# Forget gate's product: from the three-pass scheme to fp32 on quarters of TensorE's columns, with VectorE's chain split behind two k tiles and a third PSUM slot for the turnings

## The reference, cut to what matters

```
def run_layer(x, pos, ...):
    h = rmsnorm(x, norm_mix_g)
    z = h @ w_in
    u_pool = z[..., COL_POOL:COL_SSM]
    u_ssm = z[..., COL_SSM:COL_Q]
    q = z[..., COL_Q:COL_K].reshape(bn, L, FOX_HEADS, FOX_HEAD_DIM)
    k = z[..., COL_K:COL_V].reshape(bn, L, FOX_HEADS, FOX_HEAD_DIM)
    v = z[..., COL_V:COL_F].reshape(bn, L, FOX_HEADS, FOX_HEAD_DIM)
    logf = jax.nn.log_sigmoid(z[..., COL_F:COL_GATE].astype(jnp.float32)
                              + b_f.astype(jnp.float32))
    ...
    c_all = jnp.cumsum(logf_all, axis=1)
```

## Time and profile before

| | us |
|---|---|
| three runs | 1794.1, 1788.59, 1792.3 |
| median | 1792.3 |
| the profiled execution, its own time | 1792.1 |
| its span (first to last instruction of the trace) | 1790.3 |
| mean granted TensorE clock | 0.991 of full speed |
| busy in the span | PE 97%, PEld 93%, DVE 70%, ACT 36%, POOL 37% |

### The profile page before, as it was taken

The page is one execution under the profiler, slowest core; times in us unless marked ns, Lnnn a source line. Parts: engine busy times, 40 slices in busy tenths (PEclk is TensorE's granted clock), DMA queues, the critical chain, the costliest instruction groups (busy, mean ns, idle before and its releaser), DMA issues.

```text
span 1790.3 us, 31528 instructions
## 1 busy us (share of the span) xinstructions
PE 1738.6 (97%) x12453; PEld 1673.7 (93%) x12453; DVE 1246.4 (70%) x1913; ACT 641.5 (36%) x1234; POOL 668.2 (37%) x471
## 2 busy tenths in 40 slices
PE   7999999999998999999999989999999999999997
PEld 7999999888878989989999979999999999999997
DVE  6788663676775577553574589777777777698685
ACT  4210013565652222251002344444444444534343
POOL 4554334333354667413223223555544454000000
PEclk9999999999999999999999999999999999999999
DMA  8634728665634554366546331322222221998252
GB/s 275 184 123 131 235 99 251 173 174 155 177 98 139 137 115 93 90 194 216 181 133 188 95 105 37 93 89 73 73 73 73 73 73 62 348 345 284 89 189 89
DMA packets 249316, 260.69 MB, mean 146 GB/s; under 512 B 50674, under 2 KB 202974, under 8 KB 248723
## 3 DMA queue, kind: packets, MB, share of 16 engines
q1 hardware_dynamic: 235042, 227.49, 42.8%
q10 hardware_dynamic: 14128, 31.21, 4.9%
HBM read 178.09 MB, written 76.09 MB: 142 GB/s over the span
## 4 chain that ended last, share of the span: by engine, by line
PE 53%; DVE 6%; DMA 4%; issue 3%; ACT 2%; POOL 1%; SPq 0%; POOLq 0%; ACTq 0%; DVEq 0%
PE bank L156 49%; DMA act_raw<-act_scratch 2%; DMA down_raw<-in_w_down 2%; PE bank L1951 1%; PE bank L2762 1%; PE bank L1966 0%; DVE x_forms L3039 0%; PE bank L1971 0%; DVE merged L2252 0%; DMA gate<-gate_scratch 0%; DVE conv L3119 0%; POOL up_forms L2603 0%; PE bank L1936 0%; DVE xt L3009 0%; DVE prod L2245 0%
## 5 line engine op out<-in xcount | busy, mean ns | idle before, releaser
L156 PE MATMUL bank<-act_hi,w_hi 128*128 128x364 f32 (+1 forms) x1296 | 438.0, 338 | 5.2 <-DVE act_lo L2130 2.2
L156 PE MATMUL bank<-act_lo,w_hi 128*128 128x364 f32 (+1 forms) x1296 | 427.3, 330 | 0.0
L156 PE MATMUL bank<-act_hi,w_lo 128*128 128x364 f32 (+1 forms) x1296 | 426.7, 329 | 0.0
L156 PEld LDWEIGHTS bank<-act_hi,w_hi 128*128 128x128 f32 x1296 | 245.0, 189 | 20.5 <-issue 12.1
L156 PE MATMUL bank<-x_forms,up_forms 128*128 128x272 f32 x1848 | 258.4, 289 | 3.6 <-DVE part_v L3087 2.0
L156 PEld LDWEIGHTS bank<-x_forms,up_forms 128*128 128x128 f32 x1848 | 242.2, 188 | 4.7 <-DVE up_forms L3071 2.3
L156 PEld LDWEIGHTS bank<-act_lo,w_hi 128*128 128x128 f32 x1296 | 245.1, 189 | 0.1
L156 PEld LDWEIGHTS bank<-act_hi,w_lo 128*128 128x128 f32 x1296 | 244.7, 189 | 0.0
L156 PE MATMUL bank<-act_form,down_form 128*128 128x272 f32 x1848 | 233.2, 288 | 2.9 <-DVE down_form L3170 2.2
L156 PEld LDWEIGHTS bank<-act_form,down_form 128*128 128x128 f32 x1848 | 231.6, 188 | 3.4 <-issue 2.4
L2603 POOL TENSOR_TENSOR up_forms<-up_w_raw,up_forms 128x512 fp32r<-128x512 f32 x60 | 88.1, 1469 | 190.8 <-ACT up_forms L2818 190.8
(11 more groups left out here) (348 smaller groups left out, 2987.6 us busy)
## 6 DMA issues: line engine op xcount, KB each, us to landing
down_raw<-in_w_down SPq DMA_DIRECT2D x121, 256.0 KB, 4.4
w_raw<-in_w_in SPq DMA_DIRECT2D x44, 512.0 KB, 4.9
up_w_raw<-in_w_up SPq DMA_DIRECT2D x44, 512.0 KB, 4.9
gate<-gate_scratch ACTq DMA_DIRECT2D x24, 544.0 KB, 3.7
act_scratch<-ffn_act SPq DMA_DIRECT2D x22, 544.0 KB, 4.8
act_raw<-act_scratch SPq DMA_DIRECT2D x44, 272.0 KB, 4.9
gate_scratch<-gate_out ACTq DMA_DIRECT2D x48, 182.0 KB, 2.7
w_raw<-in_w_out SPq DMA_DIRECT2D x14, 512.0 KB, 4.4
```

What stands on the lines that cost most here:

```text
L156: mm = pe.matmul(out, w(k), x(k)[:, c0:c0 + cn], start=first and k == ks[0] and n == 0, stop=last and k == ks[-1] and n == 2, skip_group_c ...
```

## The change

- Job `f` and its 48 matmuls leave `JOBS`, and so do the high and low parts of its weights, the operation of GpSimd, the two of VectorE and the one of ScalarE that make them, and the nine VectorE operations that combine its halves.
- `forget(tokens)` computes the product in fp32 from `wf` (8 columns) and `xr`, 128 columns of frames at a time, with frame block j on column quarter j mod 4 of TensorE: blocks 0 to 3 behind `turn_x(6)`, blocks 4 to 7 and block 8 between the second and third group of tile q0. ScalarE copies the result to `f_raw` with five copies, ahead of its copies of `inv_b`.
- The gate's weights are loaded behind x's block 3 on SyncE's queue, and GpSimd scales them ahead of tile 1's multiply.
- The turnings use a third PSUM slot (`SLOT`, `FREED`). ScalarE does the rounding of blocks 3 and 6 (`ROUNDED`).
- Tile q1 computes its third group ahead of its second, and waits for `f_raw_done`.
- VectorE: `vector_turns(1, 2)` comes ahead of `slot(5)`, which is now k1; the first half of the f chain comes behind `low(k1)`, the second half behind `low(k2)`, then `vector_turns(4, 8)`, and then `slot(7)`, which is k3. ScalarE's exp and ln come behind its rounding of k1.

The core of the diff:

```
-JOBS = [("q", 0), ("q", 1), ("q", 2), ("q", 3), ("k", 0), ("f", 0), ("k", 1), ("k", 2), ("k", 3), ("v", 0), ("v", 1), ("v", 2),
+JOBS = [("q", 0), ("q", 1), ("q", 2), ("q", 3), ("k", 0), ("k", 1), ("k", 2), ("k", 3), ("v", 0), ("v", 1), ("v", 2),
...
+        SLOT, FREED, ROUNDED = (0, 1, 2, 0, 1, 2, 0, 1, 0), (0, 0, 0, 1, 2, 3, 4, 5, 7), (3, 6)
+        by_slot = [x.rearrange("p b (k c) -> p (b k) c", c=P) for x in (tr[:], acc[1][:, 0:2], acc[0][:, 1:3])]
+        by_k = [by_slot[a] for a in SLOT]
+        spread = [tr[:, 0], tr[:, 1], acc[1][:, 1]]
+        f_bank = acc[1][:, 2]
...
                 if t == 1:
+                    pool.wait_ge(wf_ld, 16)
+                    pool.tensor_tensor(wf[:], wf[:], m.gain1[:].unsqueeze(2).to_broadcast([P, KD, HEADS]), ALU.mult
+                                       ).then_inc(wf_scaled, 1)
                     pool.wait_ge(x_lo, 8)
...
-                if j >= 2:
-                    pe.wait_ge(x_lo, j - 1)
+                if j >= 3:
+                    pe.wait_ge(x_lo, FREED[j])
...
+            def forget(tokens):
+                pe.wait_ge(x_out, tokens[-1] + 1)
+                for k in range(KD):
+                    for j in tokens:
+                        (c0, cn), r0, at = TOK[j], 32 * (j % 4), j // 4 * P
+                        mm = pe.matmul(f_bank[r0:r0 + HEADS, at:at + cn], wf[:, k], xr[:, k, c0:c0 + cn], start=k == 0,
+                                       stop=k == KD - 1, tile_position=(0, r0))
+                mm.then_inc(f_mm, 1)
...
                 turn_x(5 + q)
+                if q == 1:
+                    pe.wait_ge(wf_scaled, 1)
+                    forget((0, 1, 2, 3))
             pe.wait_ge(x_lo, 6)
             group(0, 0, 1)
+            forget((4, 5, 6, 7))
+            forget((8,))
             pe.wait_ge(x_lo, 9)
             group(0, 0, 2).then_inc(tile_mm, 1)
...
-            group(1, 1, 1)
+            pe.wait_ge(f_raw_done, 1)
+            group(1, 1, 2)
             pe.wait_ge(inv_done, 3)
-            group(1, 1, 2).then_inc(tile_mm, 1)
+            group(1, 1, 1).then_inc(tile_mm, 1)
...
-                elif kind == "f":
-                    pe.wait_ge(wf_lo, 1)
-                    for g, (c0, cn) in enumerate(GROUPS):
-                        out = acc[a][0:FLO + HEADS, g, 0:cn]
-                        for k in range(KD):
-                            if k == 0:
-                                pe.matmul(out, wfhl[:, k], m.hh[:, k, c0:c0 + cn], start=True, stop=False)
-                            pe.matmul(out[0:HEADS], wfh[:, k], m.hl[:, k, c0:c0 + cn], start=False, stop=False)
-                            if k:
-                                mm = pe.matmul(out, wfhl[:, k], m.hh[:, k, c0:c0 + cn], start=False, stop=k == KD - 1)
-                    mm.then_inc(f_mm, 1)
...
+            act.wait_ge(f_mm, 3)
+            for q in range(4):
+                act.activation(f_raw[:, 0:TP].rearrange("h (a q c) -> h a q c", a=2, c=P)[:, :, q],
+                               f_bank[32 * q:32 * q + HEADS, 0:2 * P].rearrange("h (a c) -> h a c", c=P), ACT.Copy)
+            act.activation(f_raw[:, TP:T], f_bank[0:HEADS, 2 * P:2 * P + TS], ACT.Copy).then_inc(f_raw_done, 1)
...
+            tables.vector_turns(dve, (1, 2))
             slot(5)
-            dve.wait_ge(evac, 6)
+            low(("k", 1))
+            dve.wait_ge(f_raw_done, 1)
+            dve.wait_ge(cache_st, 32)
+            dve.tensor_tensor(fq[:, 0:T], f_raw[:], m.inv_b[0:HEADS], ALU.mult).then_inc(f_part, 1)
...
-            tables.vector_turns(dve, (1, 2))
             slot(6)
-            low(("k", 1))
+            low(("k", 2))
             dve.wait_ge(f_step, 2)
             dve.tensor_scalar(fq[:, 0:T], fq[:, 0:T], 0.0, None, ALU.min).then_inc(f_step, 1)
...
+            tables.vector_turns(dve, (4, 8))
             slot(7)
-            low(("k", 2))
-            tables.vector_turns(dve, (4, 8))
-            slot(8)
             low(("k", 3))
```

More of the change, by code:

```diff
@@ L879, in by_channel @@
     return gain.unsqueeze(2).to_broadcast([P, KD, P])
-JOBS = [("q", 0), ("q", 1), ("q", 2), ("q", 3), ("k", 0), ("f", 0), ("k", 1), ("k", 2), ("k", 3), ("v", 0), ("v", 1), ("v", 2),
+JOBS = [("q", 0), ("q", 1), ("q", 2), ("q", 3), ("k", 0), ("k", 1), ("k", 2), ("k", 3), ("v", 0), ("v", 1), ("v", 2),
         ("v", 3), ("u", 0), ("u", 1), ("m", 0), ("u", 2), ("m", 1), ("u", 3), ("m", 2), ("s", 0), ("s", 1), ("m", 3), ("s", 2),
         ("s", 3)]
-TILES = [job for job in JOBS if job[0] not in "fm"]
+TILES = [job for job in JOBS if job[0] != "m"]
 FIRST_TILE = {"u": 0, "s": MW, "q": 2 * MW, "k": 3 * MW, "v": 4 * MW}
@@ L921, in entry_engines @@
         ht, ramp, rcnt, fout = sb("pool_hist_t", [P, MW, C]), sb("ramp", [P, C]), sb("rcnt", [P, MW, C]), sb("fout", [P, 9, HEADS])
-        wf, wfhl = sb("wf", [P, KD, HEADS]), sb("wf_hi_lo", [P, KD, FLO + HEADS], F32R)
-        wfh, wfl = wfhl[:, :, 0:HEADS], wfhl[:, :, FLO:FLO + HEADS]
+        wf = sb("wf", [P, KD, HEADS])
+        sb("gap_wf", [P, KD * 40])
+        f_raw = nc.alloc_sbuf_tensor_at("f_raw", [HEADS, T], F32, offset=F_RAW_AT)
         bf, clf, grow = sb("bf", [HEADS, 1]), sb("clf", [P, 2, HEADS]), sb("gain_rows", [KD, P])
@@ L1073, in sync @@
             for i, job in enumerate(JOBS):
-                if job[0] not in "fm" and 4 <= tile_of[job] + 2 < len(TILES):
+                if job[0] != "m" and 4 <= tile_of[job] + 2 < len(TILES):
                     load_w(tile_of[job] + 2)
@@ L1163, in turn_x @@
                 pe.wait_ge(x_ld[j % 4], 16 * (j // 4) + 16)
-                if j >= 2:
-                    pe.wait_ge(x_lo, j - 1)
+                if j >= 3:
+                    pe.wait_ge(x_lo, FREED[j])
                 for k in range(KD):
-                    mm = pe.transpose(by_k[j % 2][:, k, 0:cn], xtok[0:cn, j % 4, k * P:(k + 1) * P], m.ident[0:cn, 0:cn])
+                    mm = pe.transpose(by_k[j][:, k, 0:cn], xtok[0:cn, j % 4, k * P:(k + 1) * P], m.ident[0:cn, 0:cn])
                 mm.then_inc(x_turned, 1)
@@ L1390, in vector @@
             for j, (c0, cn) in enumerate(TOK):
-                x, hi = by_k[j % 2][:, :, 0:cn], m.hh[:, :, c0:c0 + cn]
-                dve.wait_ge(x_out, j + 1)
-                dve.tensor_copy(hi, x).then_inc(x_hi, 1)
-                dve.wait_ge(x_hi, j + 1)
+                x, hi = by_k[j][:, :, 0:cn], m.hh[:, :, c0:c0 + cn]
+                if j in ROUNDED:
+                    dve.wait_ge(x_hi_act, ROUNDED.index(j) + 1)
+                else:
+                    dve.wait_ge(x_out, j + 1)
+                    dve.tensor_copy(hi, x).then_inc(x_hi, 1)
+                    dve.wait_ge(x_hi, j + 1 - sum(r < j for r in ROUNDED))
                 dve.tensor_tensor(m.hl[:, :, c0:c0 + cn], x, hi.bitcast(F32), ALU.subtract).then_inc(x_lo, 1)
@@ L1406, in scaled @@
                 a = i % 2
-                if kind == "f":
-                    dve.wait_ge(f_mm, 1)
-                    dve.wait_ge(cache_st, 32)
-                    for g, (c0, cn) in enumerate(GROUPS):
-                        ins = dve.tensor_copy(fe[:, c0:c0 + cn], acc[a][FLO:FLO + HEADS, g, 0:cn])
-                    ins.then_inc(f_part, 1)
-                    dve.wait_ge(f_part, 1)
-                    for g, (c0, cn) in enumerate(GROUPS):
-                        ins = dve.tensor_tensor(fe[:, c0:c0 + cn], acc[a][0:HEADS, g, 0:cn], fe[:, c0:c0 + cn], ALU.add)
-                    ins.then_inc(f_part, 1)
-                    dve.wait_ge(f_part, 2)
-                else:
-                    dve.wait_ge(tile_mm, tile_of[JOBS[i]] + 1)
+                dve.wait_ge(tile_mm, tile_of[JOBS[i]] + 1)
                 if kind == "u":
@@ L1436, in scaled @@
                 for g, (c0, cn) in enumerate(GROUPS):
-                    if kind == "f":
-                        ins = dve.tensor_tensor(fq[:, c0:c0 + cn], fe[:, c0:c0 + cn], m.inv_b[0:HEADS, c0:c0 + cn], ALU.mult)
-                    else:
-                        ins = dve.scalar_tensor_tensor(out=z[:, z_of[JOBS[i]] % 2, c0:c0 + cn], in0=acc[a][:, g, 0:cn],
-                                                       scalar=HD ** -0.5 if kind == "q" else 1.0,
-                                                       in1=m.inv_b[:, c0:c0 + cn], op0=ALU.mult, op1=ALU.mult)
+                    ins = dve.scalar_tensor_tensor(out=z[:, z_of[JOBS[i]] % 2, c0:c0 + cn], in0=acc[a][:, g, 0:cn],
+                                                   scalar=HD ** -0.5 if kind == "q" else 1.0,
+                                                   in1=m.inv_b[:, c0:c0 + cn], op0=ALU.mult, op1=ALU.mult)
                 ins.then_inc(evac, 1)
@@ L1573, in vector @@
             tables.vector_turns(dve, (32,))
+            slot(9)
+            tables.vector_turns_end(dve)
             slot(10)
-            tables.vector_turns_end(dve)
+            tables.vector_b(dve)
             slot(11)
-            tables.vector_b(dve)
             slot(12)
-            slot(13)
             dve.wait_ge(nc_st, 48)
```

(1 more changed line is left out.)

48 lines of the change are left out of this document (20 added, 28 removed).

## The result

| | median us | runs | ratio to the kernel before, 95% interval |
|---|---|---|---|
| before | 1791.1 | 1788.6 to 1794.1 | |
| after | 1803.9 | 1802.4 to 1805.6 | 1.0064 [1.0044, 1.0084] |

The change makes the kernel 12.8 us slower; the forecast was 1808, within 1793 to 1813. The profiled execution took 1804.15 us, 12.05 more than that of before.

What follows compares the result with a forecast made beforehand. TensorE, busy 97% of the span, and its waits for VectorE were taken as the bound. 1792.1 - 7.95 + 2.3 - 0.6 + 7.0 + 10.7 + 4.6 = 1808.2, forecast 1808 us, range 1793 to 1813.

Steps and rivals of the forecast that it cites:

- What bounds the kernel: In the edited stretch, TensorE's matmul time and its waits for VectorE set the time, microsecond for microsecond.
- The removed product: Ahead of k0's transposes, dropping the f job's 48 matmuls saves 7.95 us, as nothing waits in between.
- The fp32 product: Among turnings and q0, the added product costs 5.0 us with quarters overlapping; 15.2 if they do not.
- The turnings: At the front, the third slot wins 1.7 and 1.0 us; with the fp32 product net +2.3, bounds +1 and +5.
- The first wait: TensorE waits 7.0 us for the copy of k0's part 0, from 2.3 by order alone to 7.6 with GpSimd.
- The second wait: Before k2's part 0 is transposed, TensorE waits 10.7 us for k1's last copy; bounds 3.0 and 10.7.
- Half clock: Behind the two long waits TensorE runs at half clock, costing 3.4 to 5.8 us, taken as +4.6.
- The sum: Whole kernel: all terms added to the profiled 1792.1 us give 1808.2, forecast 1808, 0.9% slower.
- The rule on SBUF: VectorE operations with two SBUF inputs and GpSimd exclude each other for a whole instruction; both waits near upper ends, 18 us.

Runs made afterwards that it cites:

- own_order: Changed kernel with the f chain's first half ahead of slot(5), vector_turns(1, 2) behind low(k1), vector_turns(4, 8) behind low(k3); 1786.9 us, ratio 0.9978.
- turns48_behind: Changed kernel with vector_turns(4, 8) behind slot(7) and low(k3), and three later table steps each one tile later; 1794.4 us, ratio 1.0016.
- pool_holds: Changed kernel, VectorE's order untouched, GpSimd's rounding of k3's weights held until k1's evacuation and of v1's until k3's; 1794.8 us, ratio 1.0013.
- turns12_behind: Changed kernel with only vector_turns(1, 2) moved, behind slot(5) in place of ahead of it; 1796.9 us, ratio 1.0037 to the kernel before.
- squares_early_hold2: Changed kernel with all 44 GpSimd squares behind tile 6's multiply and k3's weight rounding held until k1 is evacuated; 1799.3 us, ratio 1.0035.
- two_slots: The own_order kernel with the two PSUM slots of before and every block rounded on VectorE; 1787.5 us, ratio 0.9978 to the kernel before.

## Why the prediction held, point by point

- **What bounds the kernel**: right. The time moved with TensorE's waits: against the changed kernel the waits for L1459 are 16.1 us shorter in own_order, 10.1 in turns48_behind, 8.9 in pool_holds and 7.1 in turns12_behind, and the medians 17.0, 9.5, 9.1 and 7.0. VectorE's share of busy time is 69 or 70% in all of them.
- **The removed product, -7.95**: not measured by itself. It fits the balance: from the 1/rms matmuls to the transposes of k1 (39.69 to 121.90) the changed trace has 82.21 us where the old one has 82.47. The terms for that stretch are -7.95, + 6.48 of wait, + 1.5 of half clock and - 0.2 of old wait, -0.17 in sum against the -0.26 found.
- **The fp32 product, +5.0**: 4.6 (1.86 and 2.73, to the next start). On one quarter it is 15.1 by the same measure, beside the bound of 15.2.
- **The turnings, +2.3 net** (the fp32 product included): +1.24 in the profiled execution (30.37 and 31.61), 1.1 less than forecast, the largest error of a term. q0 began at 15.17 as forecast (15.1), and the three later waits are gone. It also ran at full clock there, where before had half clock until about 18, which cost it 0.6 us; the prediction had this in its lower bound (+1) and not in its number. In seven traces with this same opening the third group starts between 31.11 and 32.90, so +0.7 to +2.5 against the one trace of before.
- **The first wait, 7.0**: 6.48. Both parts shown: 2.09 without GpSimd's operations (2.3 was worked out), 4.4 by them (5.3 at most; the rounding ran mostly beside two memsets and held the copy at L376 for 0.6 us only).
- **The second wait, 10.7**: 10.0, of which 4.5 by GpSimd's operations (pool_holds).
- **Half clock, +4.6**: 3.8. The stretch at half clock began while TensorE still waited (the granted clock is 0.50 from 110.0 to 112.5 us and from 141 to 145), so only its last 2.9 and 4.6 us cost anything. The rows that the prediction took had waits of 3.0 and 5.5 us and stretches of 3.4 and 5.8 behind them; of the four, the longest wait does not have the longest stretch behind it.
- **The sum**: 1808 against 1803.9. The terms behind it (-7.95, +1.24, -0.6, +6.48, +10.0, +3.8) give 1805.1 on the profiled 1792.1; the trace has 1804.15. All the terms that were off were too large (the front by 1.1, the two waits by 1.2 together, half clock by 0.8), so the forecast isn't near by errors that cancel.
- **The rule on SBUF**: the rows agree with it, and the lock goes further than the kind that the prediction named. A copy and an operation with one SBUF input were held as well (L377 2.44 beside the subtraction, L1551 2.41 beside the multiply); evacuations and copies out of PSUM were not (at 122.10 and 123.44, L1441 1.42 and L1459 1.28, beside GpSimd's rounding and subtraction). It holds GpSimd too: the multiply takes 2.96 us at 125.60, where it starts while VectorE's L1449 is under way (124.70 to 126.80), and 1.90 at 105.07.

## What to carry to other kernels

When work is taken out of the engine that bounds the kernel, the next thing to read is which instructions of the other engines it had covered, and in what order they stand. Here 8 us of matmuls were taken out and 16.5 us of waits came in; with the table calls behind the copies, and half of the f chain where VectorE stood idle, 0.4 us of waits is left and the kernel is 3.6 us faster than before. A dependent chain of small SBUF operations on VectorE is a costly place for GpSimd's large ones to fall: three of them made 8.8 us out of 4.5, six made 13.1. Count all of GpSimd's operations that will be free to run there. Here moving VectorE's chain brought back more (own_order) than moving GpSimd's operations (pool_holds), which can land on the next chain (squares_early_hold2). Where products are narrow, spread their columns evenly over the quarters: it gave 0.65 us here.

## What was not expected of the hardware

Executions of one kernel spread by more than most of these edits change: own_order took 1780.7 us at a mean granted clock of 0.994 and 1791.5 at 0.991. In the opening the clock is a matter of the execution too. These are 11 to 14 and 14 to 18 us in own_order and in turns48_behind, whose instructions are the same up to there (the columns are those of the earlier trace rows):

```profile
11.00:14.00 3.00, 2.84 (x15) 2.35 (x13) 2.97 (x3) 3.00 (x5) 2.02 (x1) 1.00 1.01 384
14.00:18.00 4.00, 3.31 (x24) 3.29 (x25) 3.11 (x4) 4.00 (x7) 0.30 (x1) 1.00 0.92 278
```

```profile
11.00:14.00 3.00, 2.01 (x16) 1.56 (x15) 2.93 (x4) 3.00 (x5) 2.39 (x2) 1.00 1.01 387
14.00:18.00 4.00, 3.09 (x12) 3.04 (x13) 3.65 (x4) 3.22 (x6) 0.29 (x1) 0.60 1.04 298
```

The second has a granted clock of 0.60 from 14 to 18 us, and its q0 reaches the third group at 32.90 in place of 31.13. Ahead of that TensorE was idle for more of the time (busy for 2.01 us of the three from 11 to 14, against 2.84): it waited 0.57 and 1.32 us for low parts where own_order waited 0.85 once, and just before that, at 10.85, 0.57 us for the DMA of a block of x. The column PEclk can miss such a stretch: it says 1.00 for two_slots from 14 to 18 us, where the matmuls from 17.18 start 0.30 us apart, as at half clock, and not 0.17. A single profiled execution can be 2 us off in this stretch, more than the 1.1 by which the term for the turnings was.
